# Three pairs of operand tiles moved so that each pair begins 128 bytes apart modulo 256

## The reference, cut to what matters

```python
# first block, entry: both streams, 1024 -> 5504 columns (5632 with padding)
z_x = split_cols(h_x @ w_in[l]);  z_c = split_cols(h_c @ w_in[l])
...
# first block, merge: 1024 -> 1024
merged = jax.nn.sigmoid(gate_a) * (y_a @ proj_a) + jax.nn.sigmoid(gate_b) * (y_b @ proj_b)
return merged @ w_out
...
# second block, entry of each of its two layers: 1024 -> 7424 columns (with padding)
```

## The kernel before, in words

| projection | activations mod 256 | weights mod 256 | weights minus activations |
|---|---|---|---|
| w_in | 0 | 192 | 192 |
| close | 128 | 192 | 64 |
| x (both layers) | 192 | 0 | 64 |

## Time and profile before

### The profile page before, as it was taken

How to read it: one execution, slowest core, us unless ns; L and a number is a source line. 1 busy time by engine, 2 the same in 40 slices (tenths; PEclk the granted TensorE clock), 3 DMA queues, 4 the chain that set the end, 5 groups by cost and what they waited for, 6 DMA issues and landing times. The chain is left out here.

```text
span 2798.9 us, 45371 instructions
## 1 busy us (share of the span) xinstructions
PE 2481.4 (89%) x18054; PEld 1756.3 (63%) x18054; DVE 1983.6 (71%) x4149; ACT 1147.8 (41%) x2253; POOL 690.9 (25%) x609
## 2 busy tenths in 40 slices
PE   7998877999999999999987777789999999777787
PEld 5897776788888799875543333349998555333332
DVE  5567876689999566677777777655767777777765
ACT  4345654378887545432221222235543222222222
POOL 0001110000005000034444444410001445444442
PEclk9999999999999999999999999999999999999999
DMA  7651001389998443679999999974357999999997
GB/s 312 262 211 32 4 4 39 124 325 369 370 374 328 172 155 138 267 307 421 418 421 421 421 421 421 421 307 162 136 219 279 419 420 420 421 422 421 421 421 309
DMA packets 123239, 835.50 MB, mean 299 GB/s; under 512 B 15562, under 2 KB 20844, under 8 KB 22676
## 3 DMA queue, kind: packets, MB, share of 16 engines
q0 software_dynamic: 77696, 563.91, 48.9%
q1 hardware_dynamic: 45332, 268.69, 25.3%
HBM read 831.23 MB, written 1.05 MB: 297 GB/s over the span
## 5 line engine op out<-in xcount | busy, mean ns | idle before, releaser
L3481 PE MATMUL bank<-uv_rows,z_o 128*128 128x512 f32 x872 | 420.4, 626 | 88.3 <-ACT z_o L3556 88.2
L3907 DVE CUSTOM_DVE_ANT_0 uv_rows<-uv_rows,ring 128x1024 f32<-128x1024 f32 x218 | 265.3, 1224 | 144.2 <-DMA uv_rows<-in_peer_uv,peer_index 144.1
L3481 PEld LDWEIGHTS bank<-uv_rows,z_o 128*128 128x128 f32 x872 | 167.4, 198 | 309.6 <-issue 190.0
L3341 POOL DMA_INDIRECT uv_rows<-in_peer_uv,peer_index x218 | 251.7, 1155 | 390.0 <-PE bank L3481 253.9
L3481 PE MATMUL bank<-query_weights,z_o 128*128 128x512 f32 x544 | 261.2, 627 | 62.9 <-ACT z_o L3556 62.9
L3548 ACT ACTIVATE peer_gelu<-peer_act 128x4 f32<-128x4 f32 (+1 forms) x138 | 28.3, 205 | 683.7 <-DVE peer_act L3907 683.7
L2046 DVE TENSOR_TENSOR moe_halves<-ring,moe_halves 128x1024 fp32r<-128x1024 f32 x240 | 285.7, 1222 | 28.1 <-ACT moe_halves L1964 25.8
L3481 PE MATMUL bank<-z_mg,z_o 128*128 128x512 f32 x528 | 253.7, 626 | 45.4 <-ACT z_o L3556 45.4
L3556 ACT ACTIVATE z_o<-square,peer_wts 128x128 f32<-128x128 f32 x512 | 164.7, 390 | 256.1 <-DVE peer_wts L3921 245.9
L1964 ACT ACTIVATE moe_halves<-ring 128x1024 fp32r<-128x1024 f32 x240 | 249.0, 1060 | 44.3 <-PE bank L154 41.3
L152 PE MATMUL bank<-x_halves,x_weights 128*128 128x256 f32 x800 | 231.9, 290 | 6.8 <-POOL x_halves L2548 3.5
(11 more groups left out here) (715 smaller groups left out, 5343.7 us busy)
## 6 DMA issues: line engine op xcount, KB each, us to landing
ring<-in_moe SPq DMA_DIRECT2D x96, 1024.0 KB, 7.0
ring<-in_w_in SPq DMA_DIRECT2D x80, 1024.0 KB, 4.9
ring<-in_mod_rows SPq DMA_DIRECT2D x16, 1024.0 KB, 4.9
ring<-in_w_out SPq DMA_DIRECT2D x12, 1024.0 KB, 9.6
ring<-in_mod_w SPq DMA_DIRECT2D x8, 1024.0 KB, 11.1
ring<-in_w_branch SPq DMA_DIRECT2D x8, 1024.0 KB, 7.8
query_weights<-in_peer_wq SPq DMA_DIRECT2D x8, 1024.0 KB, 11.9
ring<-in_peer_wq SPq DMA_DIRECT2D x6, 1024.0 KB, 6.8
```

The costliest lines, as they stand in the source:

```text
L3341: pool.indirect_dma_start(out=row(j), out_offset=None, in_=A["peer_uv"], in_offset=bass.IndirectOffsetOnAxis(ap=index[:, g, k:k + 1], axis ...
L3481: ins = pe.matmul(bank[2 * t + c][:, :], diag_of(j), row(j)[:, D + c * 512:D + (c + 1) * 512], start=False, stop=last)
L3907: dve.tensor_tensor_reduce(u, u, xtok[:, t, :], 1.0, 0.0, ALU.mult, ALU.add, acts[:, g % 2, j % TOPK:j % TOPK + 1]).then_inc(S["dots"], 1)
```

## The change

Only places move. `close_apart` shrinks from 80 to 32 floats, so `close_weights` begins 16384 + 128 bytes behind `close_halves`. A new tile of 48 floats is allocated ahead of `w_in_halves`. `x_weights` is allocated directly behind `x_halves` and `cmp_pos` (128 bytes), and the small tiles behind it. The activations keep their addresses, all weights shift, and all three distances become 128 modulo 256. No instruction, no order, no wait, no size of a transfer is changed; `close_apart` and `w_in_apart` are never read or written.

```diff
         mh = sb("close_halves", [P, 2, KT, SEQ], F32R)
-        apart = sb("close_apart", [P, 80])
+        apart = sb("close_apart", [P, 32])
         w2 = sb("close_weights", [P, 4, 2, TILE // 2], F32R)
...
                 table = local.enter_context(nc.sbuf_tensor("root_table", [P, 1], F32))
+                apart = local.enter_context(nc.sbuf_tensor("w_in_apart", [P, 48], F32))
...
         xh = sb("halves", [P, 2, KT, SEQ], F32R)
 
         pos = sb("cmp_pos", [P, 32])
+        w2 = sb("weights", [P, 4, 2, TILE // 2], F32R)
         mx = sb("nsa_max", [P, N, 2])
         rs = sb("nsa_sum", [P, N, 2])
         cm = sb("cmp_max", [P, N])
         hm = sb("gla_heads", [P, H4])
-        w2 = sb("weights", [P, 4, 2, TILE // 2], F32R)
         mask = sb("causal", [P, PAST])
```

## The result

The changed kernel is slower: **2813.57 us** (median of 5 runs, 2808.33 to 2815.29) against 2797.87 us (5 runs, 2794.90 to 2800.27) for the kernel before, ratio 1.0051 with a 95% interval of 1.0039 to 1.0062, so 11 to 17 us. Forecast were 2790.6 us and a range of 2788.5 to 2808. The profiled execution has a span of 2813.2 us against 2798.9.

What follows compares the result with a forecast made beforehand. TensorE's matmul pitch was taken to bound the three projections, gathers the PEER part. 9.9 us over fast pitch, less 0.9 for restarts and 0.5 for waits, gains 8.5: 2799.07 to 2790.6 us, range 2788.5 to 2808.

Steps and rivals of the forecast that it cites:

- What bounds the kernel: In the three projections each nanosecond of TensorE matmul pitch is kernel time; the gather-bound PEER part only starts earlier or later.
- a pattern which repeats after 128 bytes: All three projections: distance 128 acts as 0, nearly all runs settle fast; gain 8.5 us, chance 0.42.
- the prediction had left 0.9: First matmuls after some 85 restarts in the projections keep uneven steps, about 10 ns each: 0.9 us not gained.
- The weak point: That the fast level at distance 0 was seen only with 512 columns, in the experts' runs (226.7 ns).
- The starting rows: Restarts of about 0.22 us first step: 21 of 24 end fast at distance 64, 1 of 10 at 192.
- Rival 1, the mix stays: Projections: each run still settles fast or slow by chance, or distance does nothing; 2796 to 2802 us, chance 0.33.
- Rival 2, slower: Distance 128 has no fast level or rarely reaches it, mostly in x; 7.4 us, 2806.5 up to 2810, chance 0.25.
- Its upper term: All 256-column steps of the projections at distance 96's 118.7 ns: 7.4 and 3.4 more, +10.8 us.
- The other engines: ScalarE's and VectorE's writes of the halves take the same time and work ahead, costed at nothing.
- The 0.5 us for new waits: Waits on VectorE and loads that appear when TensorE is faster by 4%, taken off the gain: 0.5 us.
- The rule against it: Skill pages: TensorE reads moving and stationary operands independently and never waits, so distance has no effect; chance 0.10.

## Why the prediction was wrong

- **What bounds the kernel: right.** Pitch is kernel time in these stages, and PEER only shifted. It is not quite one for one: 8.7 us more of pitch in x cost 6.8, and 2.7 us less of it (3.3 with moving activations, less the 0.6 lost with moving weights) made the x stages 0.9 us shorter.
- **The step that failed: "that fits a pattern which repeats after 128 bytes, and then 128 acts as 0 does, the one distance whose runs all settle to the fast level".** What was fatal is the level given to 0. It settles fast only with 512 columns; with 256 it settles, just as firmly, at 120.0 ns, and the kernel at distance 0 has 24.4 us of excess; the prediction had left 0.9 for a distance that acts like it. The weak point that the prediction named was the one that broke: it carried over a level from one size of stream to another. With 256 columns 128 does come out near 0 (118.7 and 119.8 ns in x), but both are bad, so the same step with the right level for 0 would have forecast a loss. As a rule the repeat fails too: 64 and 192 look alike once settled but are reached with very different frequency (63 and 5% of x's steps), which the prediction had itself held against it, and with 512 columns 0 and 128 have 227.0 and 233.1 ns. The starting rows said more of the pattern than the settled levels did.
- **A reading that hid the pattern:** the prediction took moving weights and moving activations at one distance together. By the table, moving weights at 192 are moving activations at 64 in mirror, and w_in's run at 113.3 ns with moving weights (49% of the steps of its two runs are fast) belongs with x and not with w_in's slow ones.
- **Rival 1, the mix stays:** not for 128, where no run is fast. It describes well what happens within a good distance: close at 64 was slow before (0.8 us), fast in five of six profiled executions since then at that distance (0.1 us), though nothing in it differed, and w_in's two runs with moving weights at 192 read fast and slow, slow and fast, or both fast. The swing that it gives the kernel, 2 to 3 us, lies within the scatter of the runs.
- **Rival 2, slower: right in mechanism and place, its price too small.** It had 0.25 and 2806.5 to 2810 us; the kernel came out at 2813.6. Its upper term took the pitch of distance 96, 118.7 ns, for all 256-column steps (3760 steady ones; its own list has 3960 matmuls, 0.2 us more), +10.8 us. That is exactly x's pitch (+7.7 us with moving activations, +1.0 with moving weights), but w_in and close run at 119.3 to 120.0 ns (+3.3 where it allowed 2.2), and the 512-column matmuls, which it held at their 229, went to 233.1 (+1.0). Together 12.9. The bound was taken from runs of 16 matmuls, and nothing said that it was the worst. Also, 1263 is the number of fast steps in x with moving activations alone; moving weights add 135.
- **The range** left out the outcome for the same reason: its end was the slow level of before, not the slowest pitch that a clash can give.
- **The other engines: right.** VectorE's wait in w_in went from 1.3 to 0.7 us, and the totals of VectorE and ScalarE stayed. The 0.5 us for new waits on a faster TensorE was too little, as far as it could be seen: in the kernel that did reach the fast level in x, new waits alone took 1.2 us.
- **The rule against it.** By "SBUF — State Buffer", "Who interferes with whom", of the Trainium skill, TensorE's reads of the moving operand and of a weight load are independent of each other, and TensorE waits for no one; the prediction gave that 0.10. The runs contradict it as far as time goes: with all instructions equal, the place of the weights alone moves the mean pitch of x (activations moving) from 113.8 to 119.9 ns.

## What to carry to other kernels

Where fp32r matmuls with 256 columns and a weight load each set the pace, measure the pitch (distance of starts) before and after every change of the memory plan: here the distance of the two operands modulo 256 was worth up to 14 us in 2800, and most distances were bad, so a plan that happens to be good is easily lost. Count the distance as stationary less moving address, since exchanging the roles mirrors it. A level that is seen with one size of stream or load says nothing of another size. And a pitch that is a few per cent better in one stage is worth only what the engines around it can follow: look for the copy that is done just in time.

## What the runs showed of the hardware that was not expected

- Settled runs of 256 columns have several levels, among them 113.3, 117.8, 118.7 (steps in a cycle of five) and 120.0 ns (equal steps, or a cycle of three), at the same granted clock of 1.00. With 512 columns they are 226.7 and, at 128, 229 and 238 ns in turn (233.1 on average).
- What counts is the signed distance, stationary less moving, modulo 256: the same two tiles at 192 bytes give x 117.6 ns with the activations moving and 115.2 with the weights moving.
- Half of a load, with half of the rows written, is not half of the disturbance: it took the pitch at distance 0 from 119.8 to 114.0 ns and that at 64 from 115.3 to 117.3.
- With moving activations two distances that alternate from load to load came out better than either in one tile: 64 gives 115.3 ns, 192 gives 117.6, low halves at 192 with high ones at 64 give 113.8; with moving weights the mix gives 117.6 for 116.1.
- What is read in the memory at which moment, and so why 64 is the good distance, was not found; no run here shows it.
- Two executions of an identical stretch of the first block differed by 3 us, with a granted clock of 0.98 against 1.00 (lines of 230 to 510 us above).
